# Moving the conv half of an output projection from one stage of a hybrid layer into the stage before it

## The reference

```
u = x @ w_in                       -> q, kv_cmp, kv_slc, kv_win, gates, xin, bg, cg
attn = g0 * compressed(q) + g1 * selected_blocks(q) + g2 * window(q)      (width 1024)
conv = bg * conv3(cg * xin)                                                (width 1024)
mix  = concat(attn, conv) @ w_out                                          (2048 x 2048)
h    = layer_norm(ALPHA * x + mix)
y    = layer_norm(ALPHA * h + squared_relu(h @ w_mlp1) @ w_mlp2)
```

## Time and profile before

| what | us |
|---|---|
| median of 3 runs | 2712.2 (2711.11 to 2713.13) |
| the profiled execution's own time | 2708.59 |
| its span | 2706.8 |
| prompt's units in it | 639.6 to 795.8 |
| samples' sequences in it | 795.8 to 1079.3 |

### The profile page before, as it was taken

One profiled execution on the slowest core, in us unless ns is written; L12 is line 12 of the kernel. 1 busy time (PEld: TensorE's weight loads), 2 busy tenths in 40 slices (PEclk: granted clock), 3 DMA queues, 4 the chain that ended last, 5 costly groups with the idle time before them and its releaser, 6 DMA issues.

```text
span 2706.8 us, 51737 instructions
## 1 busy us (share of the span) xinstructions
PE 2593.7 (96%) x20061; PEld 2477.8 (92%) x20061; DVE 2004.7 (74%) x3181; ACT 1073.2 (40%) x1361; POOL 70.3 (3%) x118
## 2 busy tenths in 40 slices
PE   8999999998889999987999999999999999999998
PEld 8999999995657777887999999999999999999997
DVE  5788732326875555689888888888888888888898
ACT  3111111115874444455555555555433333333333
POOL 1000000000000100000000000000000000000001
PEclk9999999998999999998999999999999999999998
DMA  8776643316026775754555555555795556555642
GB/s 260 231 240 207 191 85 79 79 49 237 2 71 213 246 247 176 213 158 138 187 185 187 190 189 188 185 185 185 277 313 181 185 177 211 184 182 180 194 126 86
DMA packets 514888, 480.20 MB, mean 177 GB/s; under 512 B 49276, under 2 KB 465300, under 8 KB 503862
## 3 DMA queue, kind: packets, MB, share of 16 engines
q1 hardware_dynamic: 509722, 411.57, 48.7%
q0 software_dynamic: 4736, 67.18, 6.6%
q10 hardware_dynamic: 332, 0.11, 0.0%
HBM read 387.89 MB, written 99.16 MB: 180 GB/s over the span
## 4 chain that ended last, share of the span: by engine, by line
PE 64%; DVE 6%; ACT 3%; issue 2%; DMA 1%; SPq 1%; DVEq 0%; ACTq 0%
PE ps L2619 50%; PE ps L2535 3%; PE ps L2462 3%; PE ps L2440 2%; PE ps L2330 1%; PE ps L2400 1%; PE ps L2384 1%; PE ps L2320 1%; DVE pS L1574 1%; PE ps L2344 1%; DMA f_b<-f_scratch 1%; PE ps L2416 1%; DVE w_sl L1774 0%; ACT sS L1000 0%; ACT pT L962 0%
## 5 line engine op out<-in xcount | busy, mean ns | idle before, releaser
L1128 ACT ACTIVATE w_sh<-w_s 128x1024 fp32r<-128x1024 f32 (+1 forms) x512 | 473.6, 949 | 783.3 <-PE ps L2619 522.6
L2619 PE MATMUL ps<-f_b,w_sh 128*128 128x288 f32 x3584 | 713.8, 295 | 8.4 <-DMA f_b<-f_scratch 6.0
L1774 DVE TENSOR_TENSOR w_sl<-w_s,w_sh 128x1024 fp32r<-128x1024 f32 (+1 forms) x512 | 554.3, 1088 | 123.9 <-ACT w_sh L1128 123.5
L2619 PEld LDWEIGHTS ps<-f_b,w_sh 128*128 128x128 f32 x3584 | 574.3, 189 | 11.0 <-DMA f_b<-f_scratch 7.0
L2619 PE MATMUL ps<-f_b,w_sl 128*128 128x288 f32 x1792 | 527.1, 294 | 0.0
L2619 PE MATMUL ps<-h_u,w_sh 128*128 128x288 f32 x2560 | 514.3, 296 | 11.4 <-DVE h_u L1909 10.9
L2619 PEld LDWEIGHTS ps<-h_u,w_sh 128*128 128x128 f32 x2560 | 411.1, 189 | 12.9 <-issue 6.8
L2619 PE MATMUL ps<-h_u,w_sl 128*128 128x288 f32 x1280 | 376.6, 294 | 0.0
L2619 PEld LDWEIGHTS ps<-f_b,w_sl 128*128 128x128 f32 x1792 | 338.9, 189 | 0.0
L861 ACT ACTIVATE w_hi<-w_raw 128x2048 fp32r<-128x2048 f32 x61 | 116.9, 1916 | 484.9 <-PE ps L2171 466.3
L2171 PE MATMUL ps<-x_hi,w_hi 128*128 128x288 f32 x1408 | 302.7, 297 | 0.0
(11 more groups left out here) (322 smaller groups left out, 3340.3 us busy)
## 6 DMA issues: line engine op xcount, KB each, us to landing
w_s<-in_w_mlp SPq DMA_DIRECT2D x512, 256.0 KB, 3.7
f_scratch<-f_st SPq DMA_DIRECT2D x32, 2016.0 KB, 9.0
f_b<-f_scratch SPq DMA_DIRECT2D x56, 1152.0 KB, 8.0
w_raw<-in_w_in SPq DMA_DIRECT2D x90, 512.0 KB, 5.1
e_raw<-in_w_out SPq DMA_DIRECT2D x16, 512.0 KB, 4.3
e_raw<-in_w_out SPq DMA_DIRECT2D x64, 128.0 KB, 3.3
wb<-in_cache_win SPq DMA_DIRECT2D x8, 1024.0 KB
w_raw<-in_w_out SPq DMA_DIRECT2D x64, 128.0 KB, 2.9
```

The costliest lines, as they stand in the source:

```text
L1128: nc.scalar.activation(w_sh[m][:, :, :], blocks, ACT.Copy).then_inc(z_h[m], 1)
L1774: nc.vector.tensor_tensor(w_sl[m][:, :, :], blocks, w_sh[m][:, :, :].bitcast(F32), ALU.subtract).then_inc(z_l[m], 1)
L2619: last = nc.tensor.matmul(ps[:, bank, 0:TH], w[b][:, at_, cols], acts(k, x), start=(start and n == 0), stop=(stop and n == 2), skip_group_ ...
```

## The change

The conv half of the output projection of tokens 0 to 287 is taken out of the samples' sequences, but for 3 of its 16 blocks of output columns. The other 13 blocks are computed in the prompt's units, in 26 half steps of 12 matmuls (4 blocks of input features each), of 256 KB of weights each. In pair j (3 to 28) TensorE does one half step in two parts of 6 matmuls, one ahead of each `p_turn`. Each block's sum is copied from PSUM bank 7 by ScalarE (`c_copy`) and stored in `c_scratch`. The bank comes free because PV now uses bank 6 alone, and `p_out` adds 128 tokens at a time, 32 times, each before the next PV. The buffers of the half steps lie in the compressed branch's part of `kvn`, so their loads wait for the stores of those rows.

In the sequences, 3 conv steps stand in sequence 0, and the 16 attention steps follow: two in each of the other sequences, the second in two parts, and two at the end. `e_residual` adds the stored conv half, so it has one more VectorE instruction, and one more DMA of 144 KB for each block; its buffer is doubled. `seq_gather` issues two half gathers of 1 MB, each with its own index copy and semaphore, and each waits for its own half of the buffer only. The kept window rows are copied in 8 DMAs, one behind each of the first half steps' loads. Two small index instructions are added on VectorE and two on GpSimd in the first 20 us of the kernel.

```diff
-NE = 2 * KT
-E_FIRST = (0,) + tuple(2 + 4 * n for n in range(NB))
+CP = 13
+HS = 2 * CP
+ES = HS + KT - CP
+NE = ES + KT
+LAG = 3
+E_FIRST = (0,) + tuple(ES + 2 * n for n in range(NB - 1))
...
             def seq_gather(m):
-                if m >= 3:
-                    pool.wait_ge(t_pv, 6 * ((m - 3) // 2) + 2 * ((m - 3) % 2) + 2)
...
+                for h in range(2):
+                    q = 2 * m + h
+                    if m >= 3:
+                        pool.wait_ge(t_pv, 6 * ((m - 3) // 2) + 2 * ((m - 3) % 2) + h + 1)
+                    nc.gpsimd.tensor_copy(idx1[q % 6][:, :], idx2[:, h, m:m + 1]).then_inc(s_idx1, 1)
+                    pool.wait_ge(s_idx1, 2 * NGATH + 2 * q + 1)
+                    pool.sem_inc(s_idx1, 1)
+                    nc.gpsimd.indirect_dma_start(
+                        sg[m % 3][:, 4 * h:4 * h + 4, :].rearrange("p j c -> p (j c)"), None, slc_rows,
+                        bass.IndirectOffsetOnAxis(ap=idx1[q % 6][:, 0:1], axis=0)).then_inc(s_sgh[h][m % 3], 16)
...
+            def c_copy(n):
+                act.wait_ge(e_mm, c_step(n) + 1)
+                if n:
+                    act.wait_ge(e_tile, X_ROWS + 16 * n)
+                dst, src = c_place(n)
+                nc.scalar.activation(dst, src, ACT.Copy).then_inc(e_acc, 1)
+
+            def p_drain(u):
+                j = u // 2
+                if u % 2 and j > LAG and (j - LAG) % 2 and (j - LAG) // 2 < CP:
+                    c_copy((j - LAG) // 2)
+
+            def p_fill(u):
+                j = u // 2
+                if j == 0:
+                    mix_high(u)
+                if u % 2 and 1 <= j <= HS:
+                    e_split(j - 1)
+
             def p_act(r, last):
                 for u in range(16):
...
+                    p_drain(u + 16 * r)
                     if u + 2 < 16 or not last:
                         p_exp(u + 2, r)
+                    p_fill(u + 16 * r)
...
             def p_dve(r, last):
...
-                    if u == 3 and r:
-                        p_out(1, r - 1)
-                    if u == 11:
-                        p_out(0, r)
+                    j = u // 2 + 8 * r
+                    if u % 2 and j < 2:
+                        mix_low(j)
+                    if u % 2 and j:
+                        p_out(j - 1)
+                    if u % 2 == 0 and 2 <= j < 2 + HS:
+                        e_low(j - 2)
...
             def p_pv(j, r):
-                if j % 4 == 0:
-                    pe.wait_ge(s_of, a + 1 + 2 * r)
+                if j + 8 * r:
+                    pe.wait_ge(s_of, j + 8 * r)
...
             def p_pe(r, last):
                 for j in range(8):
+                    e = j + 8 * r - LAG
                     if j < 7 or not last:
                         p_qk(j + 1, r)
+                    if 0 <= e < HS:
+                        e_part(e, 0, 2)
                     p_turn(2 * j, r)
                     if j or r:
                         p_pv((j - 1) % 8, r if j else r - 1)
+                    if 0 <= e < HS:
+                        e_part(e, 2, 4)
                     p_turn(2 * j + 1, r)
...
                 s_pvs(b - 1, 0)
+                k_turn(b, 2)
                 s_turn(b - 1, 2)
                 s_pvs(b - 1, 1)
-                k_turn(b, 2)
-                e_step(e + 1)
                 k_qk(b, 2)
                 s_turn(b - 1, 3)
                 s_pvs(b - 1, 2)
                 s_turn(b - 1, 4)
                 s_pvs(b - 1, 3)
-                e_step(e + 2)
                 k_turn(b, 3)
-                e_step(e + 3)
+                e_part(e + 1, 0, 4)
                 k_qk(b, 3)
                 k_turn(b, 4)
+                e_part(e + 1, 4, 8)
```

More of the change, by code:

```diff
@@ L308, in build @@
         idx = const("idx", [P, NGATH], U32)
-        idx1 = [const(f"idx1{i}", [P, 1], U32) for i in range(4)]
+        p_2 = const("p_2", [P, 2])
+        idx2 = const("idx2", [P, 2, NGATH], U32)
+        idx1 = [const(f"idx1{i}", [P, 1], U32) for i in range(6)]
         h_sum = const("h_sum", [P, T])
@@ L556, in _ @@
             e_load(1)
-            load_window(0)
+            for e in range(2, HS):
+                e_load(e)
+                if e % 2 == 0 and e >= 4:
+                    c_store((e - 4) // 2)
+                if e < 2 + NB:
+                    sp.dma_start(kept[:, e - 2, :], rows_kept[:, e - 2, :]).then_inc(s_out, 16)
+            for n in range((HS - 4) // 2, CP):
+                c_store(n)
+            sp.wait_ge(s_pv, 2 + UNITS)
+            sp.wait_ge(s_of, UNITS // 2)
+            e_load(HS)
+            e_load(HS + 1)
+            sp.wait_ge(e_mm, HS)
+            load_window(0)
+            e_load(HS + 2)
+            c_store(CP)
+            e_load(ES)
+            load_window(1)
+            c_store(CP + 1)
+            e_load(ES + 1)
+            c_store(CP + 2)
+            sp.wait_ge(e_tile, X_ROWS + 16 * KT)
             e_load_x(0)
-            e_load(2)
-            e_load(3)
-            load_window(1)
+            e_load_x(1)
             for b in range(1, NB):
[L563 to L571, removed]
+                n = 2 * (b - 1)
+                e_load(ES + n + 2)
+                e_store(n)
+                e_load(ES + n + 3)
+                e_load_x(n + 2)
                 if b + 1 < NB:
                     load_window(b + 1)
+                e_store(n + 1)
+                e_load_x(n + 3)
             def out_loads(s, i, u):
@@ L1031, in _ @@
             k_copy(0, 3)
-            e_split(1)
+            c_copy(CP)
+            e_split(HS + 2)
             k_copy(0, 4)
-            e_split(2)
-            e_split(3)
+            c_copy(CP + 1)
+            e_split(ES)
+            c_copy(CP + 2)
+            e_split(ES + 1)
             for b in range(1, NB):
@@ L1041, in _ @@
                 k_copy(b, 1)
-                e_split(e + 2)
-                for g in range(3):
-                    p_copy(b - 1, g)
+                p_copy(b - 1, 0)
+                p_copy(b - 1, 1)
                 k_copy(b, 2)
-                e_split(e + 3)
+                p_copy(b - 1, 2)
                 p_copy(b - 1, 3)
@@ L1711, in _ @@
             k_max(0)
-            e_low(2)
-            e_residual(0)
+            e_low(ES)
             for b in range(1, NB):
@@ L1733, in _ @@
                 if b == NB - 1:
-                    e_low(e + 4)
-                e_residual(e // 2 + 1)
+                    e_low(e + 2)
+                e_residual(e - ES + 1)
             s_out_add(NB - 2)
```

259 lines of the change are left out of this document (152 added, 107 removed).

## The result

The changed kernel takes 2721.6 us in the median of 7 runs (2716.6 to 2726.0), the kernel before 2711.1 (2709.4 to 2713.1). The ratio is 1.0039, with an interval of 1.0028 to 1.005: slower by 0.4%, where 2703 us was forecast.

A forecast was written before the change was run, and what follows sets the result against it. TensorE's list bounds the sequences; in the units three engines hand pieces to each other. Steps -44, sequence 0 -3, gathers +5, half steps +31, mix splits +1.5 make -9.5 us: from median 2712.2 to 2703, range 2685 to 2722.

The forecast's parts named there:

- The units: Prompt's units: half steps cost 31 us and mix splits 1.5, +32.5 in all; rounds of 22.6 to 24.1 us.
- B: Rival, units: half steps paid in full, 52 us instead of 31, as units are a chain; 2724 us; chance 0.13.
- D: Rival, units: nearly all half-step work hidden, 7.4 us of a round open without weight loads; 2677 us; chance 0.15.
- What the sequences save: Seven periods lose two of four projection steps each: 46.8 us less 2.8, so -44; period 27.2 us.
- What the gathers ask: Sequence periods: half gathers make TensorE wait 0.7 us a period, +5 us in all, bounds 0 and 27.
- the line through two rows: Gathers: a line between 288 KB at 5.8 us and 2 MB at 9.8 gives 7.5 us for 1 MB.
- The lower bound of 4.9: Gathers: a 1 MB half takes at least half of a whole gather's 9.8 us, 4.9 us.
- Rival C: Periods: first half lands only when the whole did, 3.9 us wait each, 27 instead of 5; 2725 us; chance 0.10.
- SP's list: SP's DMA queue: nothing waited for stands behind a late one, save load_window behind an x load whose store has landed.
- Sequence 0: First sequence gains one step but has idle TensorE time: -3 us, bounds 3 later and 6 earlier.
- The walk past the two lists: Sequence 0: walking the two new lists past each other gave the first period 3 us earlier.
- Up to the units: Kernel's start: small index instructions lie under the first loads and cost nothing, 0 us.

The follow-up runs named there:

- the four cells above: Units' round in the changed kernel 23.2 us; with 4 of 12 half-step matmuls 21.6; with a quarter of the splits 22.9; with both edits 20.2.
- orders and loads: Changed kernel with end, part-first and sequence 0 orders edited and second step's weight loads issued earlier: 2698.7 us against 2710.0 for the kernel before, 0.9952.
- the loads moved away: Changed kernel with the second projection step's four weight DMAs issued about 3 us earlier, ahead of the store: ratio 1.0012 to the kernel before.
- the experiment on its order: Changed kernel with SyncE loading the other tokens' first weights ahead of block 13's store and block 15's x load: ratio 1.0018 to the kernel before.
- the other ten kernels: The ten follow-up edits of the changed kernel; ratios to the kernel before, where given, run from 0.9952 to 1.019.
- whole gathers: Changed kernel with only the half gathers undone, each gather 2 MB again: ratio 1.019 to the kernel before.
- three orders: Changed kernel with SyncE's end order, half-step part ahead of the waiting transpose, and sequence 0's low part ahead of scores: ratio 0.9987 to the kernel before.

## Why the prediction was wrong

**The units: right.** +32.5 forecast, +32.3 measured, round 23.2. B (over 25 us, the gaps still there) and D (under 20 us) are out: the 7.4 us of a round in which no weights are loaded, on which D rested, were not open. The reason given, that TensorE becomes the bound and the others wait for it, holds by a narrow margin only: by the four cells above, the chain through the other two engines ends 1.6 us a round behind it, and that the price came out to 0.2 us is in part luck.

**What the sequences save: right, but covered.** The steps' -44 us would make the periods 191.8; in the version with orders and loads they are 190.2, and a period is 27.0 where 27.2 was worked out.

**What the gathers ask: the step that failed most.** The room was nearly right: in the period shown the first half was issued at 900.1 and TensorE was ready at 905.6, 5.5 us, where I had 5.9. The landing was right too: 7.5 us from the line through two rows, 6.5 to 7.8 measured, 7.0 in the mean. What failed is the step from these to a price. 7.5 - 5.9 = 1.6 us a period, and I took 0.7, for no more than the thought that a light load would give less; the first halves alone cost 1.5 a period, 10.4 in all. And the second halves were to be there 9.8 us after the first issue, as two halves were taken to need no more than a whole one; they took 10.7 to 11.8, which made 3.1 us more. Together 13.5 us where 5 stood: 8.5 of the 9.3 us by which the periods missed. The lower bound of 4.9, half of the time of 2 MB, holds in no run here; with the loads moved away the shortest landing is 6.3 us, and 6.2 in the version with orders and loads. The Trainium skill ("DMA: Bandwidth & Descriptors", "Anatomy of one DMA — SWDGE (gpsimd) path") gives an estimate of 4.4 us; no run here agrees. The page gives it for one DMA, and here up to four gathers are in flight beside 512-byte packets of weights. Rival C was wrong in its condition, that a half lands only with the whole, and in its 3.9 us a period; but its sign, a wait of over 1 us in each period, came true in all seven, and half of its price.

A term was missing beside it: what TensorE does after a wait. Behind the two longest waits (2.26 and 1.99 us) its granted clock was 0.50, 3.4 us for what takes half of that, so 1.7 us in each; behind the waits of up to 1.5 us the periods were 28.6 to 29.1. The same stood in sequence 0, where the third conv step starts with matmuls 0.24 us apart, and at the end, where it is the larger part of the miss. By the rows of the sequences as a whole the clock was 0.99 before and 0.95 after; 0.01 of 283.5 us and 0.05 of 261.5 are 3 and 13 us, an estimate to which the rounding of the two rows gives a few us either way.

**SP's list: a wrong sentence.** "In its list nothing that is waited for stands behind a late one" looked at weights, x and windows of the steps, not at the first load of the next stage. That now stands behind the store of block 13 and the load of x for block 15, both of which wait for steps late in sequence 7. No term stood for the end; it cost 5.6 us, 2.4 of it in waits and 3.2 in the lower clock, and the experiment on its order gives 5.5 back.

**Sequence 0: wrong sign.** -3 forecast, within -6 to +3; +2.2 measured. The walk past the two lists missed that VectorE's low part of the third conv step stood behind the scores of chunk 3. With this one instruction moved it is -2.0, so the walk was nearly right for the rest.

**Up to the units: open.** +1.5 us, and 639.4 to 642.8 in the other ten kernels, with the same code there as the changed one. The +1.5 lies inside the scatter of single executions; whether the small instructions at the start have a share in it was not tried.

The misses are 9.3 + 5.6 + 5.2 + 1.5 - 0.2 = 21.4 us, from -9.5 to +11.9. Three of them are waits, with the clock behind them, that an order of instructions or loads makes and another removes; the split of the gain (44) and the price (32) held, and the version with the orders put right is 0.5% faster, close to what the forecast said of this one.

## What to carry to other kernels

When work is taken out of a full list, price what was hidden under it: the time between the issue of a transfer and its first reader shrinks by just what is removed. Take that transfer's time from rows with as many bytes in flight, and count half a transfer as about three quarters of a whole one (7.0 against 9.5 us here). Where a line through two rows gives a price, don't talk it down without a third row. Walk each queue through the boundary to the next stage, not only through the stage that changes: the first load of the next stage cost 5.6 us here, at one place.

When a profile gives the landing time of a group, see how many of its transfers it covers before two kernels are compared by it.

Two engines that are both nearly full in a stage hide each other: taking work from one alone gives little, so a test on one can't name the bound.

## What was not expected of the hardware

- A 1 MB gather, the first of a pair, is there 6.5 to 7.8 us after its issue, one of 2 MB 9.2 to 9.9 us: twice the bytes for some 2.5 us.
- After a wait of 6.4 to 7.0 us TensorE worked for 3.3 to 6.1 us at the lower clock level (transposes of 1.94 us instead of 1.06, matmuls 0.24 apart). In the run with whole gathers this cost an estimated 11 us beside 32.9 us of added waits.
- The length of the wait alone doesn't say whether the clock falls. In the run with three orders TensorE waited 1.97 us for scores twice; behind the first wait the clock stayed at 1.00, behind the second it was 0.70 over 5.7 us:

```profile
979.12:983.10 3.98, 3.98 (x44) 3.13 (x46) 3.30 (x7) 0.97 (x2) 1.16 (x2) 1.00 0.29 72
1007.28:1013.00 5.72, 5.72 (x46) 4.70 (x48) 3.69 (x7) 1.32 (x2) 1.36 (x2) 0.70 0.54 129
```
